# Compressed attention placed inside the steps of the attention that follows it

## What is computed

```python
kc = rms_norm_2(compress(kv_heads(kcr), cmp_pos_k, cmp_w1_k, cmp_w2_k), k_cmp_norm_g)
vc = compress(kv_heads(vcr), cmp_pos_v, cmp_w1_v, cmp_w2_v)
# compress: 31 windows of 32 tokens, + pos, @ w1 (2048 -> 256), gelu, @ w2 (256 -> 64)
...
o_cmp = softmax(q @ kc.T, masked) @ vc          # queries without rope, 31 keys
o_slc = softmax(rope(q) @ rope(k_slc).T) @ v_slc
o_win = softmax(rope(q) @ rope(k_win).T) @ v_win
attn  = (g0 * o_cmp + g1 * o_slc + g2 * o_win) * silu(z_a)
y = gelu(s5_mixer(u));  y = y * sigmoid(y @ glu_w + glu_b)
ssm = y * silu(z_s)
out = x + gate * (concat([attn, ssm]) @ w_out)
```

## Time and profile before

| | us |
|---|---|
| median of 3 runs | 1639.64 |
| lowest, highest | 1639.21, 1646.55 |
| the profiled execution | 1639.6 |
| its span, first to last instruction | 1637.8 |
| TensorE busy | 1461.7 (89%) |
| VectorE busy | 966.7 (59%) |
| ScalarE busy | 479.3 (29%) |
| mean granted TensorE clock | 0.935 of 2.4 GHz |

### The profile page before, as it was taken

How to read it: one execution, slowest core, us unless ns; L and a number is a source line. 1 busy time by engine, 2 the same in 40 slices (tenths; PEclk the granted TensorE clock), 3 DMA queues, 4 the chain that set the end, 5 groups by cost and what they waited for, 6 DMA issues and landing times.

```text
span 1637.8 us, 19815 instructions
## 1 busy us (share of the span) xinstructions
PE 1461.7 (89%) x7670; PEld 1117.3 (68%) x7670; DVE 966.7 (59%) x1649; ACT 479.3 (29%) x767; POOL 16.2 (1%) x11
## 2 busy tenths in 40 slices
PE   5998988896899888799899999999798997859998
PEld 4757888784577665687688888888477754446753
DVE  6259767655366767774546645533693648268840
ACT  5256322331322003323423432432213221114410
POOL 0000000000000000000000000000000011000000
PEclk9999999997999778899899999999898999969999
DMA  5112111221222100452134444123321112500001
GB/s 224 65 52 87 55 39 52 90 94 64 90 78 78 41 8 33 152 190 102 71 141 155 167 154 156 53 106 121 94 74 51 64 66 81 203 24 1 1 1 51
DMA packets 39885, 140.56 MB, mean 86 GB/s; under 512 B 13040, under 2 KB 17520, under 8 KB 27248
## 3 DMA queue, kind: packets, MB, share of 16 engines
q1 hardware_dynamic: 34608, 130.52, 22.2%
q10 hardware_dynamic: 5184, 8.78, 1.5%
HBM read 128.41 MB, written 8.39 MB: 84 GB/s over the span
## 4 chain that ended last, share of the span: by engine, by line
PE 53%; DVE 5%; issue 1%; ACT 1%; SPq 1%; DMA 0%; ACTq 0%; DVEq 0%; POOL 0%; POOLq 0%
PE turn L677 22%; PE score L662 7%; PE score L677 5%; PE sum L662 4%; PE turn L662 3%; PE sum L677 2%; PE sum L1205 2%; PE score L1110 1%; PE score L1179 1%; PE turn L1191 1%; SPq L603 1%; PE turn L1083 0%; DVE work L1740 0%; PE score L1236 0%; PE score L1150 0%
## 5 line engine op out<-in xcount | busy, mean ns | idle before, releaser
L1740 DVE TENSOR_TENSOR ring_r<-ring,heads_r 128x1024 fp32r<-128x1024 f32 (+3 forms) x153 | 176.3, 1152 | 216.8 <-ACT heads_r L1289 181.4
L1289 ACT ACTIVATE heads_r<-ring 128x1024 fp32r<-128x1024 f32 (+3 forms) x153 | 153.4, 1002 | 240.8 <-DMA ring<-wstream 103.1
L677 PE MATMUL score<-h_sb_r,heads_r 128*128 128x512 f32 x376 | 152.0, 404 | 0.0
L677 PE MATMUL turn<-tiles_r,heads_r 128*128 128x512 f32 x336 | 132.1, 393 | 0.0
L677 PE MATMUL turn<-h_sb_r,heads_r 128*128 128x512 f32 x304 | 119.5, 393 | 8.1 <-DVE ring_r L1740 8.1
L677 PE MATMUL turn<-wide_r,heads_r 128*128 128x512 f32 x312 | 121.9, 391 | 0.0
L677 PE MATMUL turn<-wide_r,ring_r 128*128 128x512 f32 x312 | 121.6, 390 | 0.0
L677 PE MATMUL score<-x_sb_r,heads_r 128*128 128x512 f32 x256 | 109.5, 428 | 8.2 <-DVE ring_r L1740 5.8
L677 PE MATMUL score<-x_sb_r,ring_r 128*128 128x512 f32 x256 | 104.3, 407 | 0.0
L677 PEld LDWEIGHTS score<-h_sb_r,heads_r 128*128 128x128 f32 x376 | 74.3, 197 | 14.7 <-issue 0.2
L677 PEld LDWEIGHTS turn<-tiles_r,heads_r 128*128 128x128 f32 x336 | 63.9, 190 | 13.3
(11 more groups left out here) (398 smaller groups left out, 2912.0 us busy)
## 6 DMA issues: line engine op xcount, KB each, us to landing
ring<-wstream SPq DMA_DIRECT2D x95, 1024.0 KB, 4.9
ring<-wstream SPq DMA_DIRECT2D x16, 704.0 KB, 4.3
ring<-gated SPq DMA_DIRECT2D x6, 1024.0 KB, 7.0
gated<-tiles ACTq DMA_DIRECT2D x15, 256.0 KB, 2.7
gated<-probs ACTq DMA_DIRECT2D x9, 256.0 KB, 2.0
x_sb<-xT SPq DMA_DIRECT2D x4, 512.0 KB, 5.7
x_sb<-xT ACTq DMA_DIRECT2D x1, 2048.0 KB, 8.1
outT<-x_sb SPq DMA_DIRECT2D x1, 2048.0 KB, 6.3
```

Source lines behind the costliest of these rows:

```text
L677: return pe.matmul(out, a, w, **k) if moving else pe.matmul(out, w, a, **k)
L1289: step(act.activation(head_piece(p), chunk(name)[:, c:c + cols], ACT.Identity), f"head {p}")
L1740: step(dve.tensor_tensor(out, a, b, op), name)
```

## The change

The compressed attention no longer stands between the projections and the pair loop. Its scores, turns and sums on PE, its exponential on ACT and its softmax steps on DVE are written into the pair steps (scores at step 4, turns at 11 and 12, sums at 14, 15, 16 and 18, whose results DVE adds to ATT). The score banks of the pairs are shifted by one from step 4 on. Ahead of the loop, PE does the GLU products first, then the key turns, block k, the query turns, block v, and the turns of the rotated queries. SP lays y out after the load of cmp_k1, and the glu chunk comes ahead of the compressed ones. Compressed probabilities live in heads, not in probs. What is computed stays the same.

```diff
@@ plan(): order of the weight chunks
+    out += [("glu", 4 * 512)]
     out += [(f"cmp_{kv}{i}", 8 * 256) for kv in "kv" for i in range(4)]
-    out += [("glu", 4 * 512)]
@@ buffers
-    CMP_P = part(probs, 0, 2 * T)
+    CMP_P, CMP_T = part(heads, 0, 2 * T), part(heads, 2 * T, 2 * T)
...
+    CMP_AT = 4
+    def PAIR_OF(p):
+        return PAIR[(p + (p >= CMP_AT)) % 2]
@@ SP, in the loop over chunks; this block now stands ahead of the wait for the slot
-                if name == "glu":
+                if name == "cmp_k2":
                     sp.wait_ge(y_done, 4)
...
@@ PE
-            compress("k")
-            compress("v")
             w = have("glu").rearrange("p (k n) -> p k n", k=4)
...
             tally.named["used glu"] = tally.count["gemm_full"]
+            for i in range(4):
+                turn(f"k2 {i}", [(K2(i)[:, n, :], P, n * P) for n in range(NT)], (dve_step, at("k roped")))
+            compress("k")
+            for j in range(4):
+                turn(f"q {j}", [(R2[:, n, j * P:(j + 1) * P], P, n * P) for n in range(NT)], (dve_step, at("q normed")))
+            compress("v")
+            for j in range(4):
+                turn(f"qr {j}", [(QR[:, n, j * P:(j + 1) * P], P, n * P) for n in range(NT)], (dve_step, at("q roped")))
             for kv in "kv":
                 turn(f"hidden {kv}", [(HROW(kv)[0:2 * NCMP, k * P:(k + 1) * P], 2 * NCMP, 64 * k) for k in range(2)],
...
+            def compressed_scores():
+                pe.wait_ge(turn_done, at("kcT"))
+                pe.wait_ge(score_done, at(f"pair probs {2 * CMP_AT - 3}"))
+                for n in range(NT):
+                    for j in range(4):
+                        mm = pe.matmul(PAIR[CMP_AT % 2][:, 256 * n + 64 * j:256 * n + 64 * j + 64], TL[:, 14 + j, n * P:(n + 1) * P],
+                                       KCB[:, j // 2, :], start=True, stop=True)
...
+            def compressed_turn(m):
+                b = turn_bank()
+                pe.wait_ge(dve_step, at("cmp probs"))
+                for z in range(4):
+                    mm = pe.transpose(b[:, z * P:(z + 1) * P], CMP_P[:, (4 * m + z) * P:(4 * m + z + 1) * P], ident)
...
+            def compressed_sums(n):
+                b = turn_bank()
+                pe.wait_ge(turn_done, at(f"cmp probsT {n // 2}"))
+                for g in range(2):
+                    mm = pe.matmul(b[:, 256 * g:256 * g + 256], CMP_T[:, (2 * n + g) * P:(2 * n + g + 1) * P],
+                                   VB[:, 256 * g:256 * g + 256], start=True, stop=True)
...
             def pair_scores(p):
-                if p < 2:
-                    pe.wait_ge(*((dve_step, at("cmp masked")) if p == 0 else (act_step, at("cmp out 1"))))
+                if p == 0:
+                    pe.wait_ge(turn_done, at("hidden T v"))
+                elif p == 1:
+                    pe.wait_ge(gemm_done, at("have vcmp"))
+                elif p == CMP_AT + 1:
+                    pe.wait_ge(dve_step, at("cmp masked"))
...
             for p in range(32 + 2):
+                if p == CMP_AT:
+                    compressed_scores()
...
+                if p == 2:
+                    turn("kc", [(KC2[0:NCMP, g, :], NCMP, 32 * g) for g in range(2)], (dve_step, at("kc normed")))
+                if p in (11, 12):
+                    compressed_turn(p - 11)
+                if p in (14, 15, 16, 18):
+                    compressed_sums((14, 15, 16, 18).index(p))
@@ ACT: tanh of zs, glu, tanh of za and the branch gates stand ahead of the hidden gelus; the outputs go
-            act.wait_ge(dve_step, at("cmp less max"))
-            step(act.activation(CMP_P, CMP_P, ACT.Exp), "cmp exp")
-            for z in range(2):
-                act.wait_ge(sum_full, at(f"cmp summed {2 * z + 1}"))
-                step(act.activation(work[:, 2 * z * T:2 * (z + 1) * T], sums_[:, :] if z == 0 else PAIR[1], ACT.Identity), f"cmp out {z}")
...
+                if i == 2 * CMP_AT + 5:
+                    act.wait_ge(dve_step, at("cmp less max"))
+                    step(act.activation(CMP_P, CMP_P, ACT.Exp), "cmp exp")
@@ DVE: ahead of the pairs now blocks, zs, kT copies, branch logits, q rotation, "ssm out", q copies, ...
+            def compressed(p):
+                if p == 0:
+                    dve.wait_ge(gemm_done, at("have vcmp"))
...
+                    ts(stat[:, 32:34], stat[:, 32:34], 1.0 / 64, EPS, ALU.mult, ALU.add, name="mean kc")
+                if p == 1:
+                    dve.wait_ge(pool_step, at("rstd kc"))
...
+                if p == 2:
...
+                if p == CMP_AT + 1:
+                    step(dve.tensor_reduce(m32, s3, AX.X, ALU.max))
+                if p == CMP_AT + 2:
+                    tt(s3, s3, m32.unsqueeze(2).broadcast_to([P, 32, CSLOT]), ALU.subtract, "cmp less max")
+                if p == CMP_AT + 4:
+                    dve.wait_ge(act_step, at("cmp exp"))
+                    tt(s4, s4, ck.unsqueeze(2).broadcast_to([P, NT, 8, CSLOT]), ALU.mult)
+                if p == CMP_AT + 5:
...
+                if p == CMP_AT + 6:
+                    tt(s3, s3, r32.unsqueeze(2).broadcast_to([P, 32, CSLOT]), ALU.mult, "cmp probs")
+                if p in (11, 12):
+                    take_turn(f"cmp probsT {p - 11}", CMP_T[:, (p - 11) * T:(p - 10) * T])
+                if p in (14, 15, 16, 18):
...
+                    step(dve.tensor_tensor(ATT[:, n, :], U[m % 2][:, :], ATT[:, n, :], ALU.add), f"cmp added {n}", turn_done)
@@ DVE, pair_finish: the first attention writes ATT, nothing is added to
-                t_ = part(wide, 4200 + 256 * g, 256)
+                dst = ATT[:, n, 256 * g:256 * g + 256]
+                t_ = part(wide, 4200 + 256 * g, 256) if a_ else dst
...
-                tt(dst, dst, t_, ALU.add, f"pair added {i}")
+                if a_:
+                    tt(dst, dst, t_, ALU.add, f"pair added {i}")
```

More of the change, by code:

```diff
@@ L1199, in pair_sums @@
                     if i < 8:
-                        pe.wait_ge(act_step, at("cmp out 0"))
+                        pe.wait_ge(*((y_done, 4) if i == 0 else (gemm_done, at("have vcmp"))))
                     else:
@@ L1576, in _ @@
                 pass
-            for kv in "kv":
-                drain(HROW(kv)[0:2 * NCMP, :], f"hidden {kv}", func=ACT.Gelu_apprx_tanh, cols=256, rows_=2 * NCMP)
             tzs = h_sb[:, 0:4 * T]
@@ L1582, in _ @@
                 drain(H[:, 4 + j, :], f"glu {j}", func=ACT.Tanh, scale=0.5, bias=GLUB[:, j:j + 1])
+            act.wait_ge(dve_step, at("zs gated"))
+            step(act.activation(h_sb[:, 0:4 * T], tiles[:, 6 * T:10 * T], ACT.Tanh), "tanh za")
+            act.wait_ge(dve_step, at("branch logits"))
+            for z in range(3):
+                step(act.activation(GB[z], GB[z], ACT.Tanh, scale=0.5), "branch gates" if z == 2 else None)
+            for kv in "kv":
+                drain(HROW(kv)[0:2 * NCMP, :], f"hidden {kv}", func=ACT.Gelu_apprx_tanh, cols=256, rows_=2 * NCMP)
             drain(KCRAW[0:NCMP, :], "have kc", cols=P, rows_=NCMP)
@@ L2421, in _ @@
                         take_turn(f"pair probsT {i}", PROBT(i)[:, 0:k_], cols=k_)
+                compressed(p)
                 if p in (23, 27, 31):
```

141 lines of the change are left out of this document (57 added, 84 removed).

## The result

| | before | changed |
|---|---|---|
| median of the runs, us | 1641.95 | 1628.28 |
| profiled execution, us | 1639.64 | 1629.17 |
| its span, us | 1637.8 | 1627.4 |
| its mean granted clock | 0.935 | 0.931 |

The ratio is 0.990, with a 95% interval from 0.988 to 0.992; a second set beside the experiments gave 0.9903 (0.9881 to 0.9924). The change is faster, by some 14 to 16 us. The forecast was 1609.5 us with a range from 1602 to 1619: right in its sign, 19 us too low, and outside its range. The other 4 come from the base: the forecast was made against an execution of 1639.6 us, one of the shorter ones of the kernel before, whose median is 1641.95 us here and 1643 to 1646 us beside the experiments.

What follows compares the result with a forecast made beforehand. TensorE was taken as busiest, with the thin stretch between projections and pair steps as the place to gain. -44.5 us up to the first pair step and +14.2 in the steps gave -30.3 from 1639.6: 1609.5 us, range 1602 to 1619.

Steps and rivals of the forecast that it cites:

- y laid out, GLU products: Front: y lands at 1373.9 under the projections, GLU products run 1374.4 to 1388.2; without that cover the wait costs 12 us.
- the term of -44.5: Everything up to the first pair step: first pair maximum on DVE at 1431.5 instead of 1476.01 us.
- block v +13.8: Front, behind the query turns: block v takes 13.8 us, ending at 1425.1; block k likewise 13.8.
- Steps 0 to 4: First pair steps: table load and compressed values +1.5, norm of the small keys +0.9, compressed scores and mask +3.3 us.
- I take 3.5, since the steps ran at 1.00: Step 4: the 32 pieces of compressed scores take 3.5 us at full clock, not the row's 7.1 at half clock.
- Steps 5 to 7: Pair steps: two softmax passes on DVE at 1.25 us, in return for saved 256-column adds of 0.42 us; +1.3 us.
- Steps 8 to 11: Pair steps: DVE softmax work and a copy make 5.2 us, less two adds 0.9 and old idle 0.4; +3.9 us.
- Steps 12 to 18 and behind: Late pair steps: TensorE's turn and three compressed sums +3.0 us, step 18 and the add saved at 17 +0.3.
- DVE's copy and adds fit beside it: Steps 12 to 17: TensorE sets the pace, so only its turn and sums count, +3.0 us.
- A: Rival: TensorE's clock slips in the front and shortest steps, +4 to +8 us, 1614 to 1618; chance 0.18.
- B: Rival: pair steps pay inserted work in full, each DVE insertion being late for the next copy; 1616 us; chance 0.10.
- D: Rival: DVE's insertions make TensorE pause in every step and hold its clock down; +43, 1652 us; chance 0.03.

Runs made afterwards that it cites:

- e1_front_alone: Kernel before with only the front reordered (weights, y, GLU products, turns), compressed attention still in one piece ahead of the steps; ratio 0.9943 against before.
- e4_y_late: Changed kernel with y's sixteen transfers one chunk later in SP's order, behind the load of cmp_k2; ratio 0.9971 against before.
- e5_ssm_later: Changed kernel with DVE's four GLU gatings behind the query turns' copies instead of ahead; one execution, 245.75 us from the projections' end (changed kernel 247.87).
- e12_warm_front: Changed kernel with dummy products on TensorE in the front only, none within steps 0 to 3; ratio 0.9894 against before.
- e3_warm: Changed kernel with dummy products on TensorE where it stood still, in the front and within steps 0 to 3; ratio 0.9852 against before.
- e6_exp_early: Changed kernel with a one-column exponential issued early so ScalarE's table loads while it waits; one execution, steps 0 to 4 in 15.90 us (changed kernel 17.18).
- e2_bank: Changed kernel with compressed turns and sums issued between a step's scores and its sums, not behind the pair turns; ratio 0.9872 against before.
- e11_again: Changed kernel, unedited, measured and profiled a second time beside the experiments; ratio 0.9903 against before.
- e13_nowarm_at8: Changed kernel with compressed scores at step 8, turns and sums between scores and sums, gatings behind query turns' copies, table loaded early, no dummies; ratio 0.9800 against before.
- e9_bank_at8: Changed kernel with compressed attention four steps later (scores at step 8), turns and sums between scores and sums, no dummies; ratio 0.9835 against before.

## Why the prediction was wrong

**What bounds the kernel, and the sign.** Right. The thin part in front was the place, and what was gained there outweighs what the steps pay. Front alone and moved attention bring 8 and 7 us, or 10 and 6 without the dip in the stages of e1_front_alone.

**y laid out, GLU products.** Right. The transfers came at 1366.5 on the gelu's heels, the products began with no gap, and e4_y_late puts 11.5 us on it where the text said 12.

**Query turns, blocks: the term of -44.5 measured -40.4.** The step that failed is "block v +13.8" and its twin: the forecast saw the pauses in the turns and took the blocks behind them at full clock. They took 15.24 and 15.71 us, 3.3 more than forecast for the two (14.03 each at full clock). The last products took 1.83 us, where they take 1.07 at full clock. A pause of 1 to 2 us was costed at its own length, and here it cost that and the dip behind it: e5_ssm_later took 1.1 us of pause away and gained 3.9.

**Steps 0 to 4: +5.7 measured +10.5.** The failed step is "I take 3.5, since the steps ran at 1.00". The clock was read from the steps of the kernel before and used for other steps. Before, 8 us of turns and sums without a gap came ahead of them, and TensorE was busy for 4.3 of their first 5 us. Now they begin behind short turns and waits, with the clock already down, and hold a table load and the norm of the small keys themselves; in e12_warm_front, where the clock was up before them, TensorE is busy for 2.7 of 5 us and the clock falls in them. The scores took 6.93 us, 3.4 of the 4.8 missed; the rest is in the short pieces, at half clock as well. e3_warm shows that it is the clock. Which of the insertions makes the steps too thin is not shown: e6_exp_early took out the load alone, and there the clock had fallen in front. The table's load was right at 1.28 us (e6_exp_early).

**Steps 5 to 7: +1.3 measured +3.2.** The same cause, by way of the tail of the half clock, which is back at 1.00 only by 1463: with dummies in steps 0 to 3 the stage is 13.0 us, +1.25, which is the forecast's number.

**Steps 8 to 11: +3.9.** The number is right, in part by luck: the stage holds a dip of the clock (0.66 from 1475 to 1480) that the forecast did not have, and no run with the compressed attention at step 4 is without one.

**Steps 12 to 18 and behind: +3.3 measured +7.3.** The failed step is "DVE's copy and adds fit beside it". They do not where both turn banks are held by the pair's own turns. I had costed the work of each insertion and not the buffer that it takes. e2_bank gave 3.0 of the 4.0 back, from step 8 to the end. A small part is the price itself: a compressed sum was taken at 0.86 us, where the row that it was read from gives 0.95 at full clock (3.78 us for 8 pieces at half).

**The rivals.** A named the mechanism of at least half of the miss and was priced at 4 to 8 us. The run with dummies gained 6.6 net of what they cost, so the price was fair; its chance of 0.18 was too low, though the text itself had the half clock of the thin stage and 6 us of short turns before it. B, at 1616, has neither of the two causes, and the steps cost 24.9 us, more than the 20.7 of its bound. Missing altogether was the bank wait. With both together the miss leaves the range. The case against A rested on one window with 2.8 of 4 us busy at 1.00; e12_warm_front has 2.7 of 5 us, and 0.50 behind it. D did not come: behind 1480 the steps ran at 1.00. The Trainium skill's TensorE: Matmul & The Clock Gate (A second HAM failure mode: psum-queue depth-cycling), which was weighed under D, names short idle spells between groups of matmuls as what makes the clock swing between its rates. The trace agrees in part: the clock fell in such a stretch (2.7 of 5 us busy), but then it is one stretch of 0.50 for 20 us and 1.00 behind it, with one dip, and no swing from group to group.

**The marks set for being wrong** were a first maximum after 1437 (1440.7), over 70 us from there to step 18 (74.4) and a clock under 0.9 in it (0.84). The last two were met by what the change does. The first was met only through the 5.1 us that this execution was late: in e11_again, the same kernel, the first maximum came at 1436.0. A mark at an absolute time does not hold against such shifts. It should have counted from the end of the projections.

That e13_nowarm_at8 lands near the forecast (0.980 is some 1609 us) is no defence of it: its front is 2.6 us better than forecast, which hangs on the dip ahead of it, and it has three further edits.

## What to carry to other kernels

When work is moved to make a stage denser, read the granted clock of the stage that it will then stand in from what will come before it and from how busy TensorE will be in it, not from where it stood. In this kernel a pause of TensorE of 1 to 2 us cost two to three and a half times its length where the clock fell behind it, so price it with the dip, and place small products where dense ones surround them. For each operation that is slipped into a pipelined loop, ask which buffer it takes and who holds it at that moment, and put it where the buffer has long been free.

## What the runs showed of the hardware

- TensorE's granted clock fell behind pauses of 1.9 us and 1.5 us in an otherwise busy stretch (windows of 0.69 and 0.74), and not behind single pauses of 0.4 us (block k and v of 14.03 us each in e13_nowarm_at8). It did fall at 1437.7 in the changed kernel, behind three pauses of 0.4 us between short pieces.
- The same pause does not always bring a fall: behind the pause of 2.0 us ahead of the last products of the state space model, the clock fell in 3 of the 15 profiles of the two tables, and stayed at 1.00 in 12.
- Between 1440 and 1460 it stayed at 0.50 with TensorE busy for 18.3 of 20 us, while the first 5 us of the pair steps before had 1.00 with 4.3 us busy. In e9_bank_at8, without the compressed scores at step 4, it was back at 1.00 some 10 us behind the first maximum, with short pieces alone.
- A load of ScalarE's table cost 1.28 us on the path, and moving it took off 1.28 us.
- The same code ahead of the change ended from 1374.5 to 1382.4 us in the profiles of these runs. An effect of 3 us is better read from stages than from spans. But stages are not free of it: two profiles of the changed kernel agree within 0.13 us, and dips of the clock moved single stages of other runs by 0.9 to 1.7 us.
